# Modulation tiles of the second layer requested by GpSimd, two TensorE waits put on ScalarE's copies, and one tile in each panel

## What is computed

```
ada = silu(c) @ w_ada[l] + b_ada[l]                  # 9 * 1024 values, for c and for c_ctx
s0, sc0, g0, s1, sc1, g1, s2, sc2, g2 = split(ada, 9)
n = rmsnorm(h, norm_g[l, 0]) * (1 + sc0) + s0
h = h + 0.5 * g0 * swiglu(n, w_ffn_up[l, 0], w_ffn_down[l, 0])
n = rmsnorm(h, norm_g[l, 1]) * (1 + sc1) + s1
y, ckv, k_r = token_mix(n, ...)                      # Hyena, latent attention and FNet branches
h = h + g1 * y
n = rmsnorm(h, norm_g[l, 2]) * (1 + sc2) + s2
h = h + 0.5 * g2 * swiglu(n, w_ffn_up[l, 1], w_ffn_down[l, 1])

swiglu(x) = (silu(x @ w_gate) * (x @ w_value)) @ w_down        # hidden width 2816 = 22 blocks of 128
```

## Time and profile before

| | us |
|---|---|
| median of 3 executions | 3253.72 |
| lowest, highest | 3248.5, 3254.36 |
| the profiled execution, its own time | 3249.3 |
| its span, first to last instruction | 3247.5 |
| PE busy in it | 3046.4 (94%), 19892 matmuls |
| DVE busy in it | 2125.2 (65%) |
| ACT busy in it | 1140.3 (35%) |

### The profile page before, as it was taken

One profiled execution on the slowest core, in us unless ns is written; L12 is line 12 of the kernel. 1 busy time (PEld: TensorE's weight loads), 2 busy tenths in 40 slices (PEclk: granted clock), 3 DMA queues, 4 the chain that ended last, 5 costly groups with the idle time before them and its releaser, 6 DMA issues.

```text
span 3247.5 us, 48659 instructions
## 1 busy us (share of the span) xinstructions
PE 3046.4 (94%) x19892; PEld 2956.6 (91%) x19892; DVE 2125.2 (65%) x3521; ACT 1140.3 (35%) x1820; POOL 47.9 (1%) x92
## 2 busy tenths in 40 slices
PE   7999999998999998899898899889989999999998
PEld 4999999988999998898898899889889999999998
DVE  7666666637555668686768686864375556675665
ACT  3422222314444333332443333333144443343432
POOL 0000000000000000000000000000000000000000
PEclk9999999999999999999999999999899999999999
DMA  7265543353123423333313333324532143122222
GB/s 303 89 235 217 217 164 117 126 228 130 69 73 133 172 79 111 117 104 130 111 59 124 104 117 119 114 91 154 214 108 85 69 146 142 65 92 79 91 66 72
DMA packets 89744, 408.90 MB, mean 126 GB/s; under 512 B 10050, under 2 KB 13570, under 8 KB 68915
## 3 DMA queue, kind: packets, MB, share of 16 engines
q1 hardware_dynamic: 70752, 323.52, 28.0%
q0 software_dynamic: 9504, 56.78, 4.6%
q10 hardware_dynamic: 9266, 25.50, 2.1%
HBM read 359.46 MB, written 46.30 MB: 125 GB/s over the span
## 4 chain that ended last, share of the span: by engine, by line
PE 70%; DVE 16%; issue 4%; DMA 4%; ACT 4%; SPq 0%; DVEq 0%; ACTq 0%
PE tile_psum L741 21%; PE tile_psum L748 10%; PE misc_psum L856 9%; PE tile_psum L1211 5%; PE misc_psum L860 4%; DMA w_ada<-in_w_ada 4%; PE tile_psum L702 3%; PE misc_psum L667 2%; PE tile_psum L1215 2%; PE tile_psum L667 2%; PE tile_psum L707 2%; DVE w_ada L2198 1%; PE tile_psum L856 1%; DVE h L2246 1%; PE tile_psum L1076 1%
## 5 line engine op out<-in xcount | busy, mean ns | idle before, releaser
L741 PE MATMUL tile_psum<-n_hi,whi 128*128 128x320 f32 x1536 | 352.7, 310 | 3.6 <-issue 2.2
L741 PE MATMUL tile_psum<-n_lo,whi 128*128 128x320 f32 x1536 | 350.7, 309 | 0.0
L2075 DVE TENSOR_TENSOR wlo<-raw,whi 128x2048 fp32r<-128x2048 f32 (+4 forms) x130 | 250.5, 1930 | 140.3 <-ACT whi L1482 138.2
L741 PE MATMUL tile_psum<-x_hi,whi 128*128 128x320 f32 x1300 | 299.5, 311 | 20.0 <-DVE h L2246 14.4
L741 PE MATMUL tile_psum<-x_lo,whi 128*128 128x320 f32 x1300 | 298.0, 310 | 0.0
L741 PEld LDWEIGHTS tile_psum<-n_hi,whi 128*128 128x128 f32 x1536 | 258.4, 189 | 5.8 <-DVE n_lo L2166 3.3
L1482 ACT ACTIVATE whi<-raw 128x2048 fp32r<-128x2048 f32 (+4 forms) x130 | 209.4, 1617 | 145.1 <-DMA raw<-in_w_down 44.2
L741 PEld LDWEIGHTS tile_psum<-n_lo,whi 128*128 128x128 f32 x1536 | 258.7, 189 | 0.0
L1211 PE MATMUL tile_psum<-n_hi,whi 128*128 128x320 f32 x768 | 237.4, 320 | 10.9 <-ACT gate_out L1970 10.4
L2246 DVE SCALAR_TENSOR_TENSOR h<-tile_psum,ada_t,h 128x320 f32<-128x320 f32 (+2 forms) x408 | 154.2, 433 | 137.3 <-PE tile_psum L748 133.7
L856 PE MATMUL misc_psum<-n_hi,whi 128*128 128x320 f32 x648 | 198.7, 317 | 45.8 <-DVE hidden L2357 45.8
(11 more groups left out here) (383 smaller groups left out, 6433.7 us busy)
## 6 DMA issues: line engine op xcount, KB each, us to landing
w_ada<-in_w_ada SPq DMA_DIRECT2D x128, 512.0 KB, 5.4
raw<-in_w_up SPq DMA_DIRECT2D x72, 512.0 KB, 4.1
raw<-in_w_up SPq DMA_DIRECT2D x34, 1024.0 KB, 4.9
raw<-in_w_gate SPq DMA_DIRECT2D x24, 1024.0 KB, 4.9
raw<-in_w_down SPq DMA_DIRECT2D x29, 768.0 KB, 4.4
whi<-table_keep SPq DMA_DIRECT2D x20, 1024.0 KB, 4.7
wlo<-table_keep SPq DMA_DIRECT2D x20, 1024.0 KB, 6.9
g_keep<-gate_out POOLq DMA_DIRECT2D x48, 320.0 KB, 2.5
```

The lines of the kernel that those rows point to most:

```text
L741: pe.matmul(tps[:, t.s, m, 0:TH], blk(p, m * n + k)[0], (hi, lo)[b][:, k, tok], start=k == 0 and b == 0, stop=False)
L2075: ins = dve.tensor_tensor(lo_at(r, n)[:, 0:w], raw_at(r, n)[:, 0:w], hi_at(h_, n)[:, 0:w].bitcast(F32), ALU.subtract)
```

## The change

Four things. (1) The requests for tiles 72 to 143, those of the second layer, leave SyncE's queue and stand in GpSimd's, behind layer 0's mixer, with only their own wait (`ada_used`) and a pair of semaphores of their own (`ada_late`). (2) P6 waits for `p1_kept` in place of `sum11`, and P3 for `p5_kept` in place of `sum22`; P4 still waits for `sum22`. (3) The second down panel of a chunk is rounded and split after the last panel's hidden values, in place of between its products. (4) The plan of tiles: in the six-panel chunks of (0, 1) and (1, 0) each up panel has one tile (before: 1 0 1 0 1 0 in chunks 1 and 2, and 2 1 1 1 1 1 in chunk 3), their down panels 2 2 1 1 (before 2 2 2 2), and block (0, 0) makes two tiles fewer.

```diff
-ADA_PLAN = {(0, 0): [0, 0, 2, 2, 2, 2, 2, 2] + [2] * 4 + [2] * 8 + [2] * 4 + [2] * 6 + [1, 1, 0, 0],
-            (0, 1): [0, 0, 1, 1] + [1] * 4 + [1, 0] * 3 + [2] * 4 + [1, 0] * 3 + [2] * 4 + [2] + [1] * 5 + [0] * 4,
-            (1, 0): [0, 0, 1, 1] + [1] * 4 + [1, 0] * 3 + [2] * 4 + [1, 0] * 3 + [2] * 4 + [2] + [1] * 5 + [0] * 4,
+ADA_PLAN = {(0, 0): [0, 0, 2, 2, 2, 2, 1, 1] + [2] * 4 + [2] * 8 + [2] * 4 + [2] * 6 + [1, 1, 0, 0],
+            (0, 1): [0, 0, 1, 1] + [1] * 4 + [1] * 6 + [2, 2, 1, 1] + [1] * 6 + [2, 2, 1, 1] + [1] * 6 + [0] * 4,
+            (1, 0): [0, 0, 1, 1] + [1] * 4 + [1] * 6 + [2, 2, 1, 1] + [1] * 6 + [2, 2, 1, 1] + [1] * 6 + [0] * 4,
...
+ADA_LATE = ADA_EARLY + sum(ADA_PLAN[0, 0])
...
                     elif name == "P6":
-                        pe.wait_ge(sum11, g + 1)
+                        pe.wait_ge(p1_kept, g + 1)
                     elif name == "P7":
                         pe.wait_ge(u2_kept, g + 1)
-                    elif name in ("P3", "P4"):
+                    elif name == "P3":
+                        pe.wait_ge(p5_kept, g + 1)
+                    elif name == "P4":
                         pe.wait_ge(sum22, g + 1)
...
                 for _ in range(n):
                     t = tiles_in[0]
-                    if t == DEPTH * ADA_TILES:
+                    if t == ADA_LATE:
                         return
...
                             pool.dma_start(h[:, :, :], h_keep).then_inc(h_back, 16)
+                    if l == 0:
+                        pool.wait_ge(y_done, KT)
+                        for t in range(ADA_LATE, DEPTH * ADA_TILES):
+                            pool.wait_ge(ada_used, t - 1)
+                            pool.dma_start(adaw[:, t % 2, :], w_ada[t]).then_inc(ada_late[t % 2], 16)
...
                     silu11(g)
                     if q + 1 < n:
                         fast_group(g + 1, 2)
-                    else:
-                        round_panel()
                     keep_p5(g)
                     keep_u2(g)
...
                 silu21(g0 + n - 1)
                 hidden_hi(n - 1, slice(TH, T))
+                round_panel()
...
-                        w, arrived = adaw[:, t % 2, :], ada_in[t % 2]
+                        w, arrived = adaw[:, t % 2, :], (ada_in if t < ADA_LATE else ada_late)[t % 2]
...
                     if q + 1 < n:
                         fast_low(g + 1, 1)
                         fast_low(g + 1, 2)
-                    else:
-                        split_panel()
                     ada_step(plan[q])
...
                     hidden(n - 1, slice(j * TH, (j + 1) * TH))
                     hidden_lo(n - 1, slice(j * TH, (j + 1) * TH))
+                split_panel()
                 junk_at[0] = junk_down
```

More of the change, by code:

```diff
@@ L518, in program @@
         cols_in, cols_on, turned_out, w3_in = sem("c_cols_in"), sem("c_cols_silu"), sem("ada_turned"), [sem(f"w3_in{l}") for l in range(DEPTH)]
+        ada_late = [sem(f"ada_late_in{k}") for k in range(2)]
         ada_in, ada_used = [sem(f"ada_in{k}") for k in range(2)], sem("ada_used")
```

## The result

The changed kernel took **3137.21 us** in the median of four executions (3136.47 to 3138.15); the kernel before, now with a fourth execution, 3251.11 (3247.24 to 3254.36). The ratio is 0.965, with a 95% interval of 0.9634 to 0.9667. The forecast was 3140, its range 3131 to 3166, with 0.97 for faster. The profiled execution took 3137.54, its span is 3135.4.

A forecast was written before the change was run, and what follows sets the result against it. TensorE bounds the kernel, standing still for VectorE, whose modulation tiles were requested late behind weight requests on SyncE's queue. From 3249.3 us, 112.9 of excess go, 2 are kept and down panels add 1: 3139.4, forecast 3140, range 3131 to 3166.

The forecast's parts named there:

- The excess of 112.9 us: Nine fast chunks: time over matmuls back to back, 103.1 us with tiles and 9.8 without, all expected to go.
- Tiles in time from GpSimd: Late tiles' requests: about 22 us ahead of use in fast panels, about 8 in down panels; VectorE's tile waits become 0.
- rival 5: GpSimd's requests held up by a busy VectorE, landings over 26 us, kernel slower than before; 2 in 100.
- VectorE's 11.8 of 12.3 us: Fast panel with a tile: VectorE's own 11.8 us fit in TensorE's 12.3, 0.5 us to spare, cost 0.
- the rival on VectorE: Fast panels with a tile: VectorE becomes the bound, 0.5 us over in 36 panels, 18 us, so 3158; 14 in 100.
- The two waits: P3 and P6 in fast panels: waiting for older copies leaves VectorE up to 3.5 us late at no cost.
- A VectorE late by up to 3.5 us costs nothing: After P3, sum22 next holds up P6's low weights, needed 4.7 us after P3 begins and taking 1.2 us.
- The 2 us kept for hand-overs and P6 of the last panels: Excess kept: P1's copy behind ScalarE's rounding in chunks' last panels, 0 to 0.9 us three times, and hand-overs.
- The second down panel: Last fast panel of a chunk: rounding moves behind the last hidden values, so P7's 19.4 us of waiting go.
- The down panels' +4 - 3: Down panels: (0,1)'s update late, about 1 us in four places, +4; small stalls in third and fourth panels gone, about 3.
- the rival at the head of the down panels: VectorE also misses (0,0)'s slot, 1 to 2 us at nine chunk ends, so 3149 to 3158; 12 in 100.
- The sum: Whole kernel: 3249.3 - 112.9 + 2 + 1 = 3139.4 us, forecast as 3140.

The follow-up runs named there:

- The load runs: Changed kernel with one or two more VectorE products ahead of each late tile in fast panels: 3156.3 and 3203.9 us; two products with the old waits: 3201.9 us.
- load_two_old: Changed kernel with two more VectorE products ahead of each late tile in fast panels, and P3 and P6 waiting for VectorE's sums again: 3201.9 us.
- waits_back: Changed kernel with its two waits undone, so P6 waits for sum11 and P3 for sum22 again: 3137.7 us.
- requests_back: Changed kernel with the late tiles' requests on SyncE's queue again, the other parts kept: 3174.4 us.
- split_back: Changed kernel with the second down panel rounded and split in the old place, within the last fast panel: 3166.3 us.

## Why the prediction was right, and where its reasons were not

- **The excess of 112.9 us.** Right: 111.3 us of it are gone, and it was right to count the stretch against its matmuls back to back, not by the 79.0 us of waits alone. Most of the rest had stood behind the waits, in matmuls at the lower clock, and went with them.
- **Tiles in time from GpSimd.** Right: no wait, a lead of 21 us where 22 had been worked out. In the down panels the prediction had a lead of 8 us; eight requests there had 5.9 to 6.0, and landed in 3.6 to 4.4. No landing took over 8.5 us, where rival 5 needed 26. The runs show that this is the largest part, 71 us alone and 35 of chunk length on top of all the others.
- **VectorE's 11.8 of 12.3 us.** Right, and close: one more product of 1024 elements in a panel gives 3156, what the rival on VectorE would have given (3158).
- **The two waits.** This step failed in its reason. "A VectorE late by up to 3.5 us costs nothing" looked only at the low weights as the next limit. The load runs show 1 to 2 us per chunk, and the limit at P6 and P7, by way of ScalarE's copies: P6's stands behind a wait for VectorE's `hidden`, P7's behind one for sum11. The old waits hide as much (load_two_old). In the whole change the waits are worth nothing in the time. The forecast was not hurt, because it took the excess as a whole and did not add the waits on top; that is the luck in it. The 2 us kept for hand-overs and P6 of the last panels came as 3 x 0.45 = 1.4.
- **The second down panel.** The place was right, the 19.4 us too small: undoing it costs 29. The term held only P7's wait. The lower clock behind it costs some 8 us more, and the kernel with a tile in every panel also needs the room on VectorE, since otherwise the head of the down panels waits another 0.5 to 2.1 us in four chunks. Again it stood inside the 112.9.
- **The down panels' +4 - 3.** Measured +2.8 - 3.5. The update of (0,1) behind two tiles was seen in the right place, with 0.7 us against 0.63 to 0.80; the "say 1 with the hand-over" was not needed. The update of (0,0) was in time in all chunks, so the rival at the head of the down panels did not come.
- **The sum.** Of the profiled executions 3249.3 - 3137.5 = 111.8 us are gone, where the sum had 109.9. It is not exact all along: the changed kernel reaches its first fast chunk at 1278.8 us, 5.3 later than the kernel before at 1273.5, and gains the same amount in small steps between and behind the chunks. In the profiles of the experiments that chunk starts anywhere from 1273.9 to 1281.8, whatever was edited; in waits_back, whose kernel differs from the changed one only behind that point, it is 1274.7. So I take this as scatter of the stretch ahead and no part of the change.

## What to carry to other kernels

Before a late transfer is called slow, look at when it was requested and when its buffer came free: here the landing took 4 to 6 us in the median, late tiles or not, and what made tiles late was the request's place in a queue that is worked off in order. Measure the parts of a change both alone and taken out of the whole, since two parts that hide the same lateness show 62 us in one setting and nothing in the other. And a wait moved from one engine's result to another's gives no slack where the other engine itself queues behind the first: it gave nothing where VectorE was busy without pause, and 61 us only where VectorE itself stood still for late tiles.

## What the runs showed that was not expected

- GpSimd's requests for 512 KB landed in 4.0 us in the median and at most 8.5; the same transfers from SyncE took 5.2 in requests_back, in a window of the same work. How much of that is the queue and how much the moment of the request was not separated.
- A TensorE wait can raise VectorE's own waiting for transfers: 59.8 us became 101.5 with nothing changed but two TensorE waits.
- In the last panels of a chunk under load, a panel took what VectorE's instructions add up to, 14.2 us for 14.3, with either set of waits.
- Two stalls of the same length can cost different amounts. In split_back the clock is 0.50 behind the stall of 2.38 us in chunk 1, and stays at 1.00 behind the one of 2.47 us in chunk 2. What decides it was not looked into.
